# One of two softmax scalings moved from VectorE to GpSimd in a windowed attention stage

## What is computed

```python
s_lat = jnp.einsum("bqhgd,bkhd->bhgqk", qb, kb).astype(F32) * scale
s_lat = jnp.where(valid, s_lat, -jnp.inf)
s_ctx = jnp.einsum("bqhgd,bchd->bhgqc", qb, ck).astype(F32) * scale
m = jnp.maximum(jnp.maximum(jnp.max(s_lat, -1), jnp.max(s_ctx, -1)), sink_g)
p_lat = jnp.exp(s_lat - m[..., None])
p_ctx = jnp.exp(s_ctx - m[..., None])
den = jnp.sum(p_lat, -1) + jnp.sum(p_ctx, -1) + jnp.exp(sink_g - m)
o = jnp.einsum("bhgqk,bkhd->bqhgd", p_lat, vb) + jnp.einsum("bhgqc,bchd->bqhgd", p_ctx, cv)
return o / jnp.moveaxis(den, 3, 1)[..., None]
```

## Time and profile before

| | |
|---|---|
| median of 3 runs | 2351.5 us (2351.41 to 2355.02) |
| the execution profiled | 2356.5 us, its span 2354.7 us |
| TensorE busy over the span | 2219.0 us, 94% |
| VectorE busy | 1642.0 us, 70% |
| ScalarE busy | 886.1 us, 38% |
| GpSimd busy | 695.6 us, 30% |
| the attention stage of the fourth layer | some 55 us of the span, from 2065 to 2120 |

### The profile page before, as it was taken

The page is one execution under the profiler, slowest core; times in us unless marked ns, Lnnn a source line. Parts: engine busy times, 40 slices in busy tenths (PEclk is TensorE's granted clock), DMA queues, the critical chain, the costliest instruction groups (busy, mean ns, idle before and its releaser), DMA issues.

```text
span 2354.7 us, 31154 instructions
## 1 busy us (share of the span) xinstructions
PE 2219.0 (94%) x12440; PEld 1868.0 (79%) x12440; DVE 1642.0 (70%) x2366; ACT 886.1 (38%) x1341; POOL 695.6 (30%) x454
## 2 busy tenths in 40 slices
PE   5899999999999979999998799997999999999998
PEld 5887668778888768888998687766888888858997
DVE  6755566988677985666777685769977775685443
ACT  0413332232333332344443446762322332374444
POOL 3001110223344620112356403322323446202244
PEclk9999999989999989999999799998999999999999
DMA  8422215445564563345765452214555552713552
GB/s 271 158 81 86 67 55 178 144 160 179 179 213 160 169 184 120 95 129 162 228 201 177 129 162 72 81 45 143 179 179 200 176 196 90 154 37 113 182 185 77
DMA packets 268024, 341.14 MB, mean 145 GB/s; under 512 B 31056, under 2 KB 181464, under 8 KB 267624
## 3 DMA queue, kind: packets, MB, share of 16 engines
q1 hardware_dynamic: 266704, 334.92, 44.3%
q10 hardware_dynamic: 1176, 4.23, 0.5%
HBM read 338.04 MB, written 1.08 MB: 144 GB/s over the span
## 4 chain that ended last, share of the span: by engine, by line
PE 82%; DVE 10%; ACT 3%; issue 3%; POOL 2%; DMA 1%; SPq 0%; ACTq 0%; POOLq 0%; DVEq 0%
PE PS L674 24%; PE PS L675 23%; PE PS L676 23%; DVE bias L1641 4%; DVE w_l L1612 2%; PE PS L867 2%; PE PS L890 2%; PE PS L743 1%; PE PS L1043 1%; PE PS L877 1%; PE PS L1069 1%; POOL a_l L2184 1%; DVE work L1794 1%; DVE a_l L1808 1%; ACT w_h L1239 1%
## 5 line engine op out<-in xcount | busy, mean ns | idle before, releaser
L674 PE MATMUL PS<-a_h,w_h 128*128 128x512 f32 (+1 forms) x2808 | 974.7, 347 | 43.7 <-DVE a_l L1808 27.0
L675 PE MATMUL PS<-a_l,w_h 128*128 128x512 f32 (+1 forms) x2808 | 961.5, 342 | 0.0
L676 PE MATMUL PS<-a_h,w_l 128*128 128x512 f32 (+1 forms) x2808 | 960.7, 342 | 0.0
L1612 DVE TENSOR_TENSOR w_l<-ring,w_h 128x1024 fp32r<-128x1024 f32 (+1 forms) x416 | 575.2, 1424 | 218.7 <-ACT w_h L1239 217.9
L674 PEld LDWEIGHTS PS<-a_h,w_h 128*128 128x128 f32 x2808 | 540.3, 192 | 139.1 <-issue 60.6
L1239 ACT ACTIVATE w_h<-ring 128x1024 fp32r<-128x1024 f32 (+1 forms) x416 | 408.7, 1032 | 573.3 <-PE PS L676 521.2
L676 PEld LDWEIGHTS PS<-a_h,w_l 128*128 128x128 f32 x2808 | 540.1, 192 | 60.0
L675 PEld LDWEIGHTS PS<-a_l,w_h 128*128 128x128 f32 x2808 | 540.9, 193 | 55.9
L1641 DVE SCALAR_TENSOR_TENSOR bias<-ring,silu,bias 128x512 f32<-128x512 f32 x532 | 453.0, 906 | 4.3 <-DMA ring<-in_w_mod 0.5
L2184 POOL TENSOR_TENSOR a_l<-hid,a_h 128x2048 fp32r<-128x2048 f32 (+1 forms) x60 | 228.4, 3807 | 241.1 <-ACT a_h L1263 241.1
L2199 POOL TENSOR_TENSOR hid<-hid 128x256 f32<-128x256 f32 (+1 forms) x128 | 164.5, 1287 | 409.9 <-ACT hid L1221 409.9
(11 more groups left out here) (190 smaller groups left out, 2334.4 us busy)
## 6 DMA issues: line engine op xcount, KB each, us to landing
ring<-in_w_ff SPq DMA_DIRECT2D x64, 1024.0 KB, 5.6
ring<-in_ffn_w SPq DMA_DIRECT2D x64, 1024.0 KB, 5.5
ring<-in_w_mod SPq DMA_DIRECT2D x48, 1024.0 KB, 5.2
ring<-in_ada_w SPq DMA_DIRECT2D x48, 1024.0 KB, 5.2
ring<-in_w_in SPq DMA_DIRECT2D x42, 1024.0 KB, 5.3
ring<-in_mlstm_w_in SPq DMA_DIRECT2D x12, 1024.0 KB, 5.7
ring<-in_w_o SPq DMA_DIRECT2D x8, 1024.0 KB, 5.0
ring<-in_w_attn_out SPq DMA_DIRECT2D x4, 1024.0 KB, 5.8
```

The lines of the kernel that those rows point to most:

```text
L674: nc.tensor.matmul(out, stat[0], mov[0], start=start, stop=False, **kw)
L675: nc.tensor.matmul(out, stat[0], mov[1], start=False, stop=False, **kw)
L676: return nc.tensor.matmul(out, stat[1], mov[0], start=False, stop=stop, **kw)
L1612: V.tensor_tensor(w_l[:, n % 2, c], ring[:, split_raw[n] % SLOTS, c], w_h[:, n % 2, c].bitcast(F32), ALU.subtract).then_inc(s_wl, 1)
```

## The change

GpSimd scales the first head of each pair, VectorE only the second. GpSimd waits for the same reciprocal (`s_rinv`), raises `s_prob`, and TensorE's `pair_turn` waits for that as well as for `s_probd`. In GpSimd's queue the scalings of pairs 0 and 1 stand ahead of the rotary steps, those of pairs 2 to 5 each behind the rotary steps of chunk 4 to 7, and the others after them.

```diff
@@ -1139,6 +1139,7 @@
                     def pair_turn(v):
 
                         pe.wait_ge(s_probd, v + 1)
+                        pe.wait_ge(s_prob, x0 + v + 1)
                         if v:
                             pe.wait_ge(s_pta, x0 + v)
                         for a in range(2):
@@ -2101,10 +2102,8 @@
                         step(V.tensor_tensor(r, r, esink[:, v % 4, :], ALU.add))
                         V.reciprocal(rinv[:, v % 4, :], r).then_inc(s_rinv, 1)
                         dve.wait_ge(s_rinv, v + 1)
-                        for a in range(2):
-                            y = probs(v)[:, a, :]
-                            ins = V.tensor_scalar(y, y, rinv[:, v % 4, a:a + 1], None, ALU.mult)
-                        ins.then_inc(s_probd, 1)
+                        y = probs(v)[:, 1, :]
+                        V.tensor_scalar(y, y, rinv[:, v % 4, 1:2], None, ALU.mult).then_inc(s_probd, 1)
 
                     def pair_out(p):
 
@@ -2255,7 +2254,16 @@
                         nc.gpsimd.tensor_tensor(y, y, gate_a[:, c, 0:cols], ALU.add).then_inc(s_y03, 1)
                 elif kind in ("s_in", "s_heads"):
                     pool.wait_ge(s_aux, AUX_LANDED[3])
+
+                    def first_scaled(v):
+                        pool.wait_ge(s_rinv, v + 1)
+                        y = probs(v)[:, 0, :]
+                        nc.gpsimd.tensor_scalar(y, y, rinv[:, v % 4, 0:1], None, ALU.mult).then_inc(s_prob, 1)
+
                     for st in ph["steps"]:
+                        if kind == "s_heads":
+                            first_scaled(0)
+                            first_scaled(1)
                         for e, (_, c) in enumerate(st["extra"]):
                             r, x = rotation(c), rope_chunk(ph, c)
                             wait_unit(pool, st["u"] + st["units"] + e)
@@ -2263,6 +2271,10 @@
                             nc.gpsimd.tensor_tensor(x, x, aux[:, A_ROPE:A_ROPE + LAT], ALU.mult).then_inc(s_pool, 1)
                             pool.wait_ge(s_pool, steps[0])
                             nc.gpsimd.tensor_tensor(x, x, turned[:, r % 2, :], ALU.add).then_inc(s_rot, 1)
+                            if kind == "s_heads":
+                                first_scaled(2 + e)
+                    for v in range(6 if kind == "s_heads" else 16, 16):
+                        first_scaled(v)
                 elif kind == "m_heads":
                     mask = aux[:, A_MF:A_MF + 1024].rearrange("p (d q n) -> p d q n", d=2, q=2)
```

## The result

The changed kernel took 2364.4 us in the median of five runs (2361.45 to 2368.61), the kernel before 2352.5 us in five; the ratio is 1.0048, with a 95% interval of 1.0034 to 1.0063: 0.48% slower, 8 to 15 us. A second series gave 1.0039 (1.0026 to 1.0053), some 9 us. The forecast was 2356.8 us with a range up to 2361: the direction was right, the size half of what came.

What follows compares the result with a forecast made beforehand. It took a TensorE and ScalarE ring of 7.37 us per two pairs as the bound. Relieving VectorE gains naught; late transposes add 5.47 us, 0.2 comes back: +5.3 on the 2351.5 median gives 2356.8 us, range 2354.0 to 2361.0.

Steps and rivals of the forecast that it cites:

- the stage: The fourth layer's attention, the only part the change touches; 58.70 us before, from TensorE's first transposes to its last values product.
- The ring of TensorE and ScalarE: In the fourth layer's attention, transposes, copies, exponentials, rounding and values product in sequence: 7.37 us per two pairs, without VectorE.
- turn(1): Start of TensorE's eight transposes of pair 1, which wait for both engines' scalings; predicted 0.64 us late.
- The duration d: Length of one GpSimd scaling of 128x512; taken as 1.04 us, with bounds of 0.48 and 1.27.
- Part 2: The prediction's step sizing the 16 scalings added on GpSimd, each between 0.48 and 1.27 us.
- turn(5): Start of TensorE's transposes of pair 5, behind rotary steps and VectorE's weight split; predicted to add 2.99 us, 5.47 late altogether.
- values(2): TensorE's product with the values that follows pair 5's transposes; predicted to give 0.2 us back.
- rival B: GpSimd gets its operands first, so VectorE's scaling stands still in every pair: about +8 us, 2359.6; chance 0.10.
- Part 3: The walk through TensorE's waits pair by pair, with VectorE's 128x2 operation held until GpSimd's scaling ends; sum +5.3 us.
- C: Rival: a GpSimd scaling takes 2 us or more, transposes of pairs 2 and 4 no longer hidden; +10, 2362; chance 0.05.
- D: Rival: nothing visible happens, since TensorE's transposes had over two us of room; 2351.5 us; chance 0.03.
- From pair 6 on: No rotary step stands ahead of GpSimd's scalings; predicted covered, VectorE pulling ahead by 0.8 us in each period.

Runs made afterwards that it cites:

- e3_one_scaling: The kernel before with the scaling of each pair's first head left out and nothing added on GpSimd; ratio 1.0000, stage 58.19 us (-0.51).
- e2_late_pairs: The changed kernel with VectorE scaling both heads of pairs 0 to 5, GpSimd the first head only from pair 6; ratio 1.0006, stage +0.57 us.
- o1_odd_first: The changed kernel with GpSimd scaling pairs 3 and 5 right behind pairs 2 and 4, before the rotary steps of chunks 5 and 7; ratio 1.0007.
- e5_320_columns: The changed kernel with GpSimd scaling only 320 of the first head's 512 columns, the rest left unscaled; ratio 1.0031, stage 65.29 us (+6.59).
- w2_busy_waits: The changed kernel with 3, 4 and 6 useless matmuls filling TensorE's three long waits without delaying its transposes; ratio 1.0031, stage 65.69 us.
- s1_sine_first: The changed kernel with VectorE's weight split put behind the sine part of chunk 7 instead of ahead; ratio 1.0043, stage 69.73 us.
- a1_after: The changed kernel run again unaltered, as base of the second series and for a second profile; ratio 1.0039, stage 68.64 us (+9.94).
- e4_tt: The changed kernel with GpSimd's scaling written as a two-input product with the reciprocal repeated along the columns; ratio 1.0045, stage 67.35 us.
- b1_weights_gpsimd: The kernel before with ScalarE's four roundings and VectorE's four splits of next-phase weights moved behind GpSimd's rotary steps; ratio 1.0048, stage 69.11 us.
- e1_scale_first: The changed kernel with GpSimd's scalings of pairs 2 to 5 in front of the rotary steps of chunks 4 to 7; ratio 1.0009, stage 60.24 us.

## Why the prediction was right or wrong, point by point

**What bounds the stage: right.** The ring of TensorE and ScalarE sets the pace, at 7.37 us for two pairs before and after, though VectorE had the same 7.36 us of work back to back. `e3_one_scaling` and `e2_late_pairs` show it: taking work off VectorE gives 0.4 us at turn(1) (0.5 in all), nothing in the ring.

**The mechanism: right.** The main loss is the chain turn, rotation matmul, sine part, rotary steps, scaling, next turn. Reordering GpSimd alone took 7.0 of 8.6 us away. That the odd pairs carry it was right too, in `o1_odd_first`. With the duration that the prediction assumed, turn(2) and turn(4) were hidden as it said: in `e5_320_columns` they came 4.80 us behind the turns before.

**The duration d: wrong, the first of two terms that were mis-sized.** The upper bound of Part 2, GpSimd's two-input product at 1.27 us, was no bound. The scaling form took 1.57 alone. The bound took for granted that an operation with one tensor input can't be slower than one with two; the same multiplication as a product of two inputs takes 1.04. Nor was 1.27 the longest such row of the kernel before. Its page has another two-input product of this size, though such a mean can hold time in which the engine was held up:

```profile
L2237 POOL TENSOR_TENSOR work<-work,big 128x512 f32<-128x512 f32 x8 | 13.9, 1741 | 103.8 <-DVE big L1880 103.8
```

By `w2_busy_waits`, where the clock plays no part, the stage with 1.57 is +7.0. Turn by turn, the increase over the kernel before in us:

| | predicted, d = 1.04 | `w2_busy_waits`, 1.57 |
|---|---|---|
| turn(1) | 0.64 | 1.08 |
| turn(2) | 0 | 0.39 |
| turn(3) | 1.84 | 2.36 |
| turn(4) | 0 | 0.45 |
| turn(5) | 2.99 | 2.89 |
| values(2) | -0.2 | -0.16 |
| sum | 5.3 | 7.0 |

Turn(3) pays the longer d in full and turn(1) most of it, and turns 2 and 4 are past their cover, all as the prediction's own steps say for 1.57, to 0.1 us. For turn(5) they would say 3.6 and for the sum 7.8, and there another of its steps fails, the hold, told below.

**The clock: left out altogether, the second.** The prediction turned waits into time one for one. Behind waits of 2.2 to 2.9 us the granted clock fell, in the first profile to a mean of 0.63 over 4.6 us, and another 1.6 to 2.9 us were lost. So +7.0 and 1.6 make the stage of the first profile (8.56), +7.0 and 2.9 that of the second (9.94). That these sums close is no proof, since both clock terms are differences to `w2_busy_waits`; what shows the cause is that the slow stretches vanish with the idle time.

**What stays open.** The medians stand 11.9 us apart in the first series and the ratio of the second says 9, with half-widths of some 3. That agrees with stages of 8.6 to 11 (69.73, so 11.0, in `s1_sine_first`). The execution whose stage is +8.56 was the fastest of its five (2361.45). That the others had more slow stretches would fit, but was not shown. The forecast also stood on a median before of 2351.5 us, which is 2352.5 with all five runs.

**Who holds up whom: half right.** In the changed kernel VectorE went first where both started on the same reciprocal, 0.06 us ahead or more, and GpSimd was stretched, by 0.29 us rather than 0.48. So rival B did not come about there. But Part 3's step that VectorE's 128x2 operation is held until GpSimd's scaling ends was wrong where it was used. In the changed kernel this operation (L2094 there)

```profile
2077.57 0.16 DVE L2094 SCALAR_TENSOR_TENSOR nmax<-nmax,nsink 128x2 f32<-128x2 f32 x1
```

ran at its usual 0.16 us in the middle of the scaling of pair 3 (2076.83 to 2078.40). The step had entered the sum at turn(5): by it the sine part of chunk 7 starts 2.73 us behind turn(4), or 2.80 with a scaling of 1.57. It started 2.48 behind it in `e5_320_columns` and 2.06 in `w2_busy_waits`, where the 128x2 operation of pair 6 had its 0.16 too. So this error made the sum too long, by 0.3 us at d = 1.04 and 0.7 at 1.57, and hid a part of what d had made it too short.

There was a hold, only elsewhere. At pair 6 of the changed kernel GpSimd has two scalings back to back, from 2089.38:

```profile
2089.45 0.62 DVE L2096 TENSOR_TENSOR esink<-nmax,sink 128x2 f32<-128x2 f32 x1
...
2090.38 0.83 DVE L2106 TENSOR_SCALAR work<-work,rinv 128x512 f32<-128x512 f32 x1
2089.38 3.27 POOL L2261 TENSOR_SCALAR work<-work,rinv 128x512 f32<-128x512 f32 x2
```

The 128x2 operation, which began 0.07 us behind the scaling, was let go 0.69 us after the scaling's start (0.70 in `w2_busy_waits` and `a1_after`). Those that began 0.72 and 0.74 after it were not held at all. VectorE's own scaling began 1.00 us into GpSimd's first, which lasted until 2090.94, and ended 0.28 past its end. It cost nothing, for TensorE's next turn came later.

The Trainium skill (SBUF — State Buffer, Who interferes with whom) has an exclusive lock, in which the order of issue decides. That one engine stands still for the other, the rows of `e4_tt` and `b1_weights_gpsimd` agree with, though the 128x2 operation above was let go long before the scaling's end. On the order, the starts of the profile decide only when they are far enough apart: with VectorE 58 ns ahead or more it was never held by the scaling that began behind it, with 47 to 49 ns in half of the cases, with 44 or 45 always. So its lead of 0.03 us, which the prediction set against rival B, was no safe ground: 15 ns less than in the changed kernel went with rival B. GpSimd's form differed too between those runs and its part was not separated, but that one form, with the constant, went both ways at 47 to 49 ns speaks for the starts.

**Rivals C and D.** C took a scaling of 2 us or more. It was 1.57, 1.86 beside VectorE's, but what C said of turns 2 and 4 came true, and the time of 2364.4 us is nearer to its 2362 than to the forecast. D, nothing visible, is out by the three waits.

**The weight split ahead of the sine part: right that it costs, incomplete.** It was in the way (sine part at 2087.37, where L774 had ended at 2086.42), but `s1_sine_first` shows that moving it gains nothing.

**From pair 6 on: nearly right.** turn(6) is the exception when the pairs before it are on time: 0.45 to 0.56 us late in `e1_scale_first` and `e2_late_pairs`. In the changed kernel the delay of turn(5) covered it.

**The range: wrong.** It ended at 2361.0. The duration was outside its bounds, the clock was not considered, and both lie on the same side.

## What to carry to other kernels

An engine with 30% load is no free engine: what matters is what stands in its queue ahead of the new work, and on whom that waits. Follow the chain from one iteration to the next, for here a step moved behind another that itself depends on the previous iteration's consumer turned a hidden 1.6 us into a loss of 7. Prefer the row of the very instruction form over one with more inputs when sizing a new operation, and where a new wait leaves TensorE idle (here 2.2 to 3.1 us at a time), count a stretch at the lower clock behind it as well. And where two engines start on one semaphore, don't build on which of them gets through first: here the outcome turned over with 15 ns of difference in the starts.

## What the runs showed of the hardware that was not expected

GpSimd on a float32 tile in SBUF, alone: multiplication of 128x512 with a per-partition scalar 1.56 to 1.57 us, with a constant 1.49, the same multiplication as a product with the scalar repeated along the columns 1.04, a scaling of 128x320 1.08 to 1.09, and in `b1_weights_gpsimd` a rounding copy of 128x1024:

```profile
2085.86 1.04 POOL L2267 CAST w_h<-ring 128x1024 fp32r<-128x1024 f32 x1
```

So the copy takes about 1 ns per column, the scaling 2.5 ns (1.57 - 1.085 us over 192 columns) plus some 0.3 us. For operations with one input the Trainium skill (GPSIMD Engine Reference, Engine selection) gives about line rate. The copy agrees (1.0 ns per column, where VectorE's scaling takes 0.8, 0.40 us for 512), the scaling does not, and it is slower than the two-input product.

When the two engines' scalings started on the same reciprocal, who was held went with some 15 ns in the starts; that the form had no part in it was not shown. GpSimd's scaling form, 58 ns or more behind VectorE, was stretched by 0.2 to 0.3 us and VectorE kept its 0.49. GpSimd's two-input form, 44 or 45 ns behind, kept its 1.04 and VectorE took 1.37. The scaling form with a constant, 47 to 49 ns behind, went either way (VectorE 0.94, or GpSimd 1.79).

A rounding copy on GpSimd holds VectorE too. In `b1_weights_gpsimd` a VectorE operation on 128x2 numbers took 1.00 us (2085.92, shown above) and ended with the copy that began at 2085.86.

TensorE's clock dropped behind waits of 2.2 to 3.1 us in this stage, though not behind each of them, in some profiles once and in others twice. It stayed at 1.00 when the same waits were filled with matmuls down to 0.2 to 0.5 us, and in the kernels without them (longest wait 1.6 us).
